# A two-block transformer on one core: the mixing input projection on split weights and rows, paired latent values, and a router in four column groups

## The reference, cut to what matters

```python
# first_block, layer 0: latent attention, 8 heads, values of 64 columns
kv = jnp.einsum('bsr,rhd->bshd', rms_norm(c_kv, kv_lat_norm), w_ukv)
k_nope, v_a = kv[..., :MLA_NOPE], kv[..., MLA_NOPE:]
o_a = dense_causal_attention(q, k, v_a)
...
# second_block, layer 0: the mixing layer; w_in is 1024 x 3072, ctx has 256 rows too
h = modulate_2(rmsnorm(x, g_mix), sh1, sc1)
z = h @ w_in[i]
q, k, v = jnp.split(z[..., 3 * C_HYENA:], 3, axis=-1)      # 3 * C_HYENA = 1536
hc = modulate_2(rmsnorm(xc, g_mix), csh1, csc1)
kvc = hc @ w_in[i][:, kv_off:]                             # kv_off = 2048
kc, vc = jnp.split(kvc, 2, axis=-1)
y_na = neighborhood_attention(..., kc, vc, na_rpb[i])
y_hy = hyena_mixer(z[..., :3 * C_HYENA], *hy)              # short filter of 3 taps, long convolutions
x = x + gt1 * (jnp.concatenate([y_hy, y_na], axis=-1) @ w_mix_out[i])
...
# second_block, layer 1: mixture of 8 experts, 2 for each row
logits = (h @ w_router).astype(jnp.float32) + b_router.astype(jnp.float32)
top_val, top_idx = lax.top_k(logits, TOP_K)
```

## Time and profile before

| what | us |
| --- | --- |
| median of 3 runs (lowest to highest) | 2389.74 (2387.16 to 2394.24) |
| the profiled execution | 2388.43 |
| span in its trace | 2387.1 |
| busy: PE | 2295.7 (96%) |
| busy: DVE | 1800.2 (75%) |
| busy: ACT | 1226.5 (51%) |
| busy: POOL | 411.0 (17%) |
| mean granted clock of PE | 0.99 |
| transferred | 630.36 MB, mean 264 GB/s |

### The profile page before, as it was taken

The page is one execution under the profiler, slowest core; times in us unless marked ns, Lnnn a source line. Parts: engine busy times, 40 slices in busy tenths (PEclk is TensorE's granted clock), DMA queues, the critical chain, the costliest instruction groups (busy, mean ns, idle before and its releaser), DMA issues.

```text
span 2387.1 us, 27392 instructions
## 1 busy us (share of the span) xinstructions
PE 2295.7 (96%) x10949; PEld 1734.8 (73%) x10949; DVE 1800.2 (75%) x2024; ACT 1226.5 (51%) x1436; POOL 411.0 (17%) x447
## 2 busy tenths in 40 slices
PE   6988999999999999899999899999999999999998
PEld 2455897545599877447996588788887888788886
DVE  4756787687698855675664388989888888889897
ACT  1243653223255321334433377777767676767775
POOL 1234570134165010452220000000000000000000
PEclk9999999999999999999999999999999999999999
DMA  8633568541647874134664379989998999899995
GB/s 328 251 156 106 229 256 314 221 192 72 220 177 282 322 304 185 53 142 176 247 247 172 115 290 361 353 333 358 355 361 327 361 356 355 328 369 352 366 352 216
DMA packets 49463, 630.36 MB, mean 264 GB/s; under 512 B 7456, under 2 KB 8049, under 8 KB 11633
## 3 DMA queue, kind: packets, MB, share of 16 engines
q1 hardware_dynamic: 44192, 618.81, 68.6%
q10 hardware_dynamic: 2752, 6.99, 0.8%
q0 software_dynamic: 2384, 2.73, 0.3%
...
## 4 chain that ended last, share of the span: by engine, by line
PE 82%; DVE 10%; ACT 3%; issue 2%; DMA 2%; POOL 1%; ACTq 0%; SPq 0%; DVEq 0%
PE psum L1198 19%; PE psum L1199 19%; PE psum L1200 19%; PE psum L1064 5%; PE psum L1093 4%; PE psum L2655 3%; DVE sbuf L727 2%; DVE ring_r L1193 2%; PE psum L2658 1%; PE psum L3276 1%; DVE sbuf L1340 1%; DMA ring<-in_t_ada 1%; PE psum L2316 1%; PE psum L3176 1%; DMA ring<-in_t_mlp 1%
## 5 line engine op out<-in xcount | busy, mean ns | idle before, releaser
L1199 PE MATMUL psum<-ring_r,sc_r 128*128 128x512 f32 x1688 | 665.1, 394 | 0.0
L1193 DVE TENSOR_TENSOR ring_r<-ring,sbuf_r 128x2048 fp32r<-128x2048 f32 (+1 forms) x287 | 536.7, 1876 | 141.2 <-ACT sbuf_r L1184 139.7
L1184 ACT CAST sbuf_r<-ring 128x2048 fp32r<-128x2048 f32 (+1 forms) x287 | 445.6, 1556 | 313.3 <-PE psum L1200 255.9
L1193 DVE TENSOR_TENSOR ring_r<-ring,sc_r 128x2048 fp32r<-128x2048 f32 (+1 forms) x243 | 476.2, 1969 | 107.3 <-ACT sc_r L1184 106.5
L1184 ACT CAST sc_r<-ring 128x2048 fp32r<-128x2048 f32 (+1 forms) x243 | 398.3, 1643 | 246.6 <-PE psum L1200 224.2
L1198 PE MATMUL psum<-sbuf_r,sc_r 128*128 128x512 f32 (+1 forms) x1148 | 425.6, 371 | 3.5 <-DVE ring_r L1193 3.1
L1199 PEld LDWEIGHTS psum<-ring_r,sc_r 128*128 128x128 f32 x1688 | 316.9, 188 | 72.0 <-issue 1.4
L727 DVE SCALAR_TENSOR_TENSOR sbuf<-ring,sbuf 128x512 f32<-128x512 f32 x405 | 332.7, 828 | 15.0 <-DMA ring<-in_t_ada 9.5
L1200 PE MATMUL psum<-sbuf_r,sc_r 128*128 128x512 f32 x860 | 339.6, 395 | 0.0
L1198 PE MATMUL psum<-sc_r 128*128 128x512 f32 x828 | 331.1, 400 | 0.0
L1200 PE MATMUL psum<-sc_r 128*128 128x512 f32 x828 | 324.3, 392 | 0.0
...
## 6 DMA issues: line engine op xcount, KB each, us to landing
...
```

The source lines that it names most:

```text
L1184: p.act.e.copy(p.r(hi), src).then_inc(*p.sig("high", st.tag, n))
L1193: p.dve.e.tensor_tensor(p.r(src), src, p.r(hi), ALU.subtract).then_inc(*p.sig("lowp", st.tag, n))
L1199: e.matmul(out, l[0], r[1], start=False, stop=False)
```

## The change

Three edits, in one diff.

**The input projection of the mixing layer.** The weight is cut into 24 pieces. Pieces 0 to 19 are 8 row blocks by 128 columns, four to a tile; pieces 20 to 23 are 2 row blocks by 512 columns. ACT casts each piece into one of three buffers (`HBI`, two of which are the normed rows' own buffer `XN`), GpSimd subtracts it in place (`pool_in2`), and PE does three products where there was one. The rows `n4` and the context rows are split as well (`HTLI`, `HTCL`, `FTI`). Pieces 16 to 19 serve two units each, and pieces 20 to 23 serve all four units 12 to 15, which therefore all finish with the last piece. Unit ends are now told by `in2_done`. ACT waits for the last piece of the MLP (`piece mlp1 63`) and casts piece 0 before the norm; each later cast stands three pieces ahead in ACT's list. ACT's context turn stands behind piece 7, and its 12 activations for the short filter are dealt out over tile 3's pieces. The load of the spectra `KH` goes behind all six rounds, and POOL's seeds of the tiles 41 to 43 stand between its subtractions.

**The values of the latent attention.** The heads are paired, with four `PT` buffers, and `pe_pair_values` skips the masked half of the second key block.

**The router.** Its weights are padded to 32 columns; the eight products go to four column groups of 32, two per group. The four parts are added by the matmul that used to transpose, with a matrix `SEL` of four stacked identities that DVE makes ahead. Constant matmuls fill PE's waits. The subtraction for the rows' low parts goes from DVE to GpSimd, at the end of its list.

```diff
...
         self.mla = mla = Heads("mla", [sc[:, 13824 + 256 * i:14080 + 256 * i] for i in range(4)],
-                               [xn[:, 512 * i:512 * i + 512] for i in range(2)], [(i,) for i in range(4)], [(4,), (5,)], 3,
-                               dil.DG)
+                               [xn[:, 512 * i:512 * i + 512] for i in range(4)], [(i,) for i in range(4)], [(4,), (5,)], 3,
+                               dil.DG, pair=True)
         for h in range(8):
-            mla.causal(self, h, h % 2, QT[0:96, h, :], KT[0:96, h, :])
-            mla.rows(h, 2, 64, [KV[:, k, 128 * h + 64:128 * h + 128] for k in range(2)], v3(mla.PT[h % 2], 2), [6, 7],
+            mla.causal(self, h, h % 4, QT[0:96, h, :], KT[0:96, h, :])
+            mla.rows(h, 2, 64, [KV[:, k, 128 * h + 64:128 * h + 128] for k in range(2)], v3(mla.PT[h % 4], 2), [6, 7],
                      HT[:, h // 2, :], False)
...
         self.HTC = v3(sc[:, 11288:13336], 8)
+        self.HTLI, self.HTCL = v3(sc[:, 15236:17284], 8), v3(sc[:, 17284:19332], 8)
+        self.FTI = [sc[:, 8216 + 256 * i:8472 + 256 * i] for i in range(4)]
+        self.HBI = [sc[:, 19332:20356], XN[:, 0, :], XN[:, 1, :]]
...
         self.HBE = [sc[:, 16112:18160], sc[:, 18160:20208], self.ht, self.acc]
-        self.RWL, self.RW = sc[:, 0:64], v3(sc[:, 0:64], 8)
-        self.BR = sc[:, 64:72]
+        self.RWL, self.RW = sc[:, 0:256], v3(sc[:, 0:256], 8)
+        self.BR = sc[:, 256:264]
+        self.SEL = sc[:, 15528:15536]
...
 def turn_at(p, tag, r):
-    return p.at("turnA" if r % 2 == 0 or tag in LOW else "turnD", tag, r)
-LOW = ("n1", "n3", "n5")
+    return p.at("turnA", tag, 2 * r + 1) if tag in LOW else p.at("turnD" if r % 2 else "turnA", tag, r)
+LOW = ("n1", "n3", "n4", "n5", "ctx")
...
-def act_turn_low(p, tag, tmp, mul, add):
+def act_turn_low(p, tag, tmp, mul, add, banks=TURNS):
     for c in range(8):
...
             p.act.wait_ge(*p.at("low", tag, c - len(tmp)))
-        p.act.e.activation(tmp[c % len(tmp)], p.bank[TURNS[c // 2]][:, 256 * (c % 2):256 * (c % 2) + 256], ACT.Identity,
+        bank = p.bank[banks[c // 2 % len(banks)]]
+        p.act.e.activation(tmp[c % len(tmp)], bank[:, 256 * (c % 2):256 * (c % 2) + 256], ACT.Identity,
                            bias=add[:, c:c + 1], scale=mul[:, c:c + 1]).then_inc(*p.sig("turnA", tag, c))
...
     if f"n{s}" in LOW:
-        act_turn_low(p, f"n{s}", p.FTF if s == 5 else p.FTM, mul, add)
+        act_turn_low(p, f"n{s}", {4: p.FTI, 5: p.FTF}.get(s, p.FTM), mul, add)
     else:
...
     if f"n{s}" in LOW:
-        dve_turn_low(p, f"n{s}", p.FTF if s == 5 else p.FTM, p.HT, p.HTLF if s == 5 else p.HTLM)
+        dve_turn_low(p, f"n{s}", {4: p.FTI, 5: p.FTF}.get(s, p.FTM), p.HT, {4: p.HTLI, 5: p.HTLF}.get(s, p.HTLM))
     else:
...
         for h in pair:
-            ins = p.pe.e.matmul(p.bank[h.bank][h.r0:h.r0 + h.v[kb].shape[1], 0:256], h.v[kb], h.pt[:, kb, :],
+            q0 = 0 if (h.both or kb % 2 == 0) else 128
+            ins = p.pe.e.matmul(p.bank[h.bank][h.r0:h.r0 + h.v[kb].shape[1], q0:256], h.v[kb], h.pt[:, kb, q0:256],
                                 start=(kb == 0), stop=(kb == n - 1))
...
     return p.at("in2A" if u % 2 and not 6 <= u < 12 else "in2D", u)
+def in2_done(p, u):
+    if u < 8:
+        return p.at("piece", "win2", 2 * u + 1)
+    return p.at("piece", "win2", {10: 17, 11: 19, 15: 23}[u]) if u in (10, 11, 15) else p.at("in2", u)
+def in2_stream(p):
+    return Stream("win2", pieces(range(5), False, lambda t: 8, 512, 1024) + pieces((5,), True, lambda t: 8, 512, 1024),
+                  p.HBI, lambda t: (8, 512))
 def pe_in2(p):
-    e, HT = p.pe.e, p.HT
+    HT, HTC = (p.HT, p.HTLI), (p.HTC, p.HTCL)
+    st = in2_stream(p)
     for j in range(6):
...
+        for q in range(4):
+            n = 4 * j + q
+            hi, lo = st.parts(p, n)
+            hi, lo = p.r(hi), p.r(lo)
+            p.pe.wait_ge(*p.at("scaled", "win2", n))
+            units = (2 * j + q // 2,) if j < 4 else (8 + q // 2, 10 + q // 2) if j == 4 else (12, 13, 14, 15)
+            for u in units:
+                ps = p.bank[2 + u % 5]
+                i = u - IN2_U[j]
+                tag, rows = ("n4", HT) if i < 2 else ("ctx", HTC)
+                if u >= 5 and (q == 0 if j == 5 else q % 2 == 0):
+                    p.pe.wait_ge(*in2_at(p, u - 5))
+                if j < 5:
+                    for k in range(8):
+                        p.pe.wait_ge(*p.at("low", tag, k))
+                        ins = three(p, ps[:, 256 * (q % 2):256 * (q % 2) + 256], (hi[:, k, :], lo[:, k, :]),
+                                    [p.r(r[:, k, :]) for r in rows], k == 0, k == 7)
+                    if j == 4 and q % 2 and i < 2:
+                        ins.then_inc(*p.sig("in2", u))
+                else:
+                    b = i % 2
+                    for k in range(2 * q, 2 * q + 2):
+                        ins = three(p, ps, [p.r(r[:, k, 128 * b:128 * b + 128]) for r in rows],
+                                    (hi[:, k - 2 * q, :], lo[:, k - 2 * q, :]), k == 0, k == 7)
+                    if q == 3 and u < 15:
+                        ins.then_inc(*p.sig("in2", u))
+            ins.then_inc(*p.sig("piece", "win2", n))
         if j:
             pe_sums(p, 36 + j)
         if j == 1:
...
-def put_in2(p, E, side, j):
+def put_in2(p, E, side, units):
     banks = in2_banks(p)
-    for u in range(IN2_U[j], IN2_U[j + 1]):
+    for u in units:
         if 6 <= u < 12:
...
             if side == "A":
-                E.wait_ge(*p.at("in2", u))
+                E.wait_ge(*in2_done(p, u))
                 E.e.activation(p.r(hi), ps, ACT.Copy, scale=scale).then_inc(*p.sig("in2A", u))
...
             ps = v3(p.bank[2 + u % 5], 2) if double else p.bank[2 + u % 5]
-            E.wait_ge(*p.at("in2", u))
+            E.wait_ge(*in2_done(p, u))
             ins = E.e.tensor_copy(dst, ps) if side == "D" else E.e.copy(dst, ps)
...
 def act_mix(p):
     a, e = p.a, p.act.e
+    st = in2_stream(p)
+    p.act.wait_ge(*p.at("piece", "mlp1", 63))
+    act_high(p, st, 0)
     act_norm(p, 4)
     e.dma_start(p.CX, a["ctx_2"][0].rearrange("(b p) d -> p b d", p=128)).then_inc(*p.land("ctx_in"))
     act_modulated(p, 4)
+    p.act.wait_ge(*p.at("tp", "n4", 3))
+    act_high(p, st, 1)
+    act_high(p, st, 2)
     act_context(p)
+    p.act.wait_ge(*p.at(*mod_at(p, 2, 0, 1)))
+    p.act.wait_ge(*p.at(*mod_at(p, 2, 1, 1)))
+    for n in range(24):
+        j, q = n // 4, n % 4
+        act_high(p, st, n + 3)
+        if q % 2:
+            put_in2(p, p.act, "A", (n // 2,) if j < 4 else (8 + q // 2, 10 + q // 2) if j == 4 else
+                    (12, 13, 14, 15) if q == 3 else ())
+        if q == 3 and j:
+            act_gates(p, 36 + j)
+        if n == 7:
+            p.act.wait_ge(*p.at("low", "n4", 7))
+            act_turn_low(p, "ctx", p.FTI, p.CTXC[1], p.CTXC[0], [0, 1])
+        if j == 3:
+            if q == 0:
+                p.act.wait_ge(*in2_at(p, 4))
+                p.act.wait_ge(*in2_at(p, 5))
+                p.act.wait_ge(*p.at("shorts"))
+                p.act.wait_ge(*p.at("low", "ctx", 7))
+            for c in range(3 * q, 3 * q + 3):
+                e.activation(p.ZC[:, c, :], p.ZT[:, c, 0:256], ACT.Identity, bias=p.SB[:, c:c + 1],
+                             scale=p.SW[0][:, c:c + 1]).then_inc(*p.sig("left", c))
     p.act.wait_ge(*p.total("kept0"))
     p.act.wait_ge(*p.total("kept1"))
     e.dma_start(p.KH, p.spectra.rearrange("p (m n) -> p m n", m=5)).then_inc(*p.land("kh_in"))
-    p.act.wait_ge(*p.at(*mod_at(p, 2, 0, 1)))
-    p.act.wait_ge(*p.at(*mod_at(p, 2, 1, 1)))
-    for j in range(6):
...
     act_gates(p, 42)
     put_hz(p, p.act, "A")
     act_exp(p, p.na, 0)
...
     for j in range(6):
-        put_in2(p, p.dve, "D", j)
+        put_in2(p, p.dve, "D", range(IN2_U[j], IN2_U[j + 1]))
         dve_products(p, 8, 37 + j)
...
         if j == 1:
-            dve_turn(p, "ctx", p.HTC, 8, [0, 1], p.CTXC[1], p.CTXC[0])
+            dve_turn_low(p, "ctx", p.FTI, p.HTC, p.HTCL)
         if j == 3:
...
+def pool_in2(p):
+    st = in2_stream(p)
+    pool_seed(p, 40)
+    for n in range(24):
+        hi, src = st.parts(p, n)
+        p.pool.wait_ge(*p.at("high", "win2", n))
+        p.pool.e.tensor_tensor(p.r(src), src, p.r(hi), ALU.subtract).then_inc(*p.sig("scaled", "win2", n))
+        pool_seed(p, {12: 41, 16: 42, 20: 43}.get(n, 0))
 def pool_mix(p):
-    pool_seed(p, 43)
+    pool_in2(p)
     for i, one, two, end in steps(p.na):
...
         p.pe.wait_ge(*ht_at(p, 7, k))
-        ins = e.matmul(p.bank[2][0:8, 0:256], p.RW[:, k, :], p.HT[:, k, :], start=(k == 0), stop=(k == 7))
+        g = 32 * (k % 4)
+        ins = e.matmul(p.bank[2][g:g + 32, 0:256], p.RW[:, k, :], p.HT[:, k, :], start=(k < 4), stop=(k >= 4))
     ins.then_inc(*p.sig("logits"))
+    pe_constants(p, 6, (256,))
+    p.pe.wait_ge(*p.at("select"))
     p.pe.wait_ge(*p.at("turnedlogits"))
     for b in range(2):
```

(22 more changed lines are left out.)

40 lines of the change are left out of this document (4 added, 36 removed).

## The result

The changed kernel takes 2416.85 us (median of 4 runs, 2412.96 to 2421.47) against 2388.99 for the kernel before: 1.0107 times, 95% interval 1.0088 to 1.0126. The direction was forecast, the size was not: +27.9 us where +8.2 was predicted, and 2416.85 lies above the range's end of 2410. The profiled execution has a span of 2417.2 us against 2387.1, so 30.1 us are to be found in its trace.

A forecast was written before the change was run, and what follows sets the result against it. PE was taken to bound the kernel. Terms from -20.1 to +10.6 gave +9.7 us for the mixing stage, -1.5 latent values, 0 router: +8.2 on 2389.7, 2398 us; range 2378 to 2410.

The forecast's parts named there:

- Columns: Mixing input projection: three split products take PE less time than one float32 product, 20.1 us less.
- The shared way as exclusive: Mixing stage, path into SBUF: a two-input DVE operation waits until GpSimd's ends, and the reverse; three places cost 19.7 us.
- costs little: Rival, mixing stage: GpSimd and DVE hardly hold each other up, the three places' 19.7 us fall away; 2374 us, chance 0.20.
- Piece 11: Mixing stage, round 2: its cast waits behind ACT's context turn and DVE's context splits, so the round ends 6.7 us late.
- The tail: Mixing stage, last product to attention scores: DVE's last adaLN products come late, 7.0 instead of 2.8 us, +4.2 us.
- Router: Router: column groups and fills gain, GpSimd's row subtraction blocks DVE's small steps; 0 taken, bounds -4.3 to +2 us.
- The norm ahead of it: +3.5 us: Norm before the mixing projection: ACT waits for the last MLP piece and casts piece 0 before squaring, +3.5 us.
- Split rows: Mixing stage's start: splitting the rows delays the first piece, +2.4 us; one split held by a subtraction, another +2.4.
- place 2: Mixing stage, context split: it stands behind DVE's products for tiles 36 and 37, round 2 ends near 906, +6.7 us.
- GpSimd as bound: Rival, mixing stage: subtractions of 2.94 us are slower than PE, whose clock falls after idling; 2410 us, chance 0.15.
- Latent values: -1.5 us: Latent attention: paired heads save PE time, 0 to 2.6 us, 1.5 taken, kept because its stage sets the end.
- Place 3: Mixing stage, round 5: banks are cleared only after DVE's products and short-filter steps, PE's second unit starts late, +10.6 us.

The follow-up runs named there:

- e8: Kernel before with the mixing edit alone, DVE subtracting, its work dealt out and products a round earlier, cast of piece 0 behind the norm: 2377.81 us (0.9942).
- e4: Changed kernel with the 24 subtractions on DVE instead of GpSimd, adaLN products and short filter dealt out over pieces: 2405.15 us (1.0052).
- e11: e7 with seven of eight adaLN products left out for tiles 37 to 42: 2392.31 us (1.0006).
- e5: Changed kernel with constant matmuls in four of PE's waits of the mixing stage: 2421.68 us (1.0121).
- e6: Changed kernel with the wait for the last MLP piece and the cast of piece 0 behind the norm in ACT's list: 2413.71 us (1.0095).
- e3: Kernel before with the mixing projection edit alone: 2415.87 us (1.0100).
- e2: Kernel before with the router edit alone (column groups, fills, row subtraction on GpSimd): 2391.51 us (1.0002).
- e9: Kernel before with the paired latent values and small constant matmuls in the same loop: 2392.75 us (1.0005).
- e12: e8 and e9 in one kernel, plus the router edit with its row subtraction on DVE behind the choice of experts: 2381.14 us (0.9948).
- e1: Kernel before with the paired latent values alone: 2394.54 us (1.0016).
- e7: Changed kernel, GpSimd still subtracting, with DVE's list dealt out evenly and adaLN products a round earlier: 2410.08 us (1.0077).

## Why the prediction was wrong in size

**What held.** *Columns:* in rounds without a wait the split form runs as reckoned (e8: rounds 4 and 5 in 45.4 us against 55.4), and e8 collects 13.7 us of the 20.1 at the scores. *The shared way as exclusive:* the case on which the sign was staked. e4, e8 and e11 show it from three sides, and the rival "costs little" is out. *One subtraction:* 2.35 us predicted; the 24 take 2.35 to 2.84, half of them at most 2.41. *Piece 11:* PE waited 5.2 us for it, part of the 6.7. *The tail:* 7.2 us from the last product to the scores, 7.0 predicted. *Router:* +0.5 for 0.

The Trainium skill, SBUF — State Buffer, SBUF: two separate sides, gives the rule: whoever starts first of a GpSimd operation and a DVE operation with two SBUF inputs or in a two-port mode gets the port pair for the whole instruction. This trace agrees, with 2.77 us for a product of 0.75. Its section Who interferes with whom also names copy, cast and tensor_scalar as operations that can be such and `tensor_reduce` as never one; here the rows agree too (1.97 for 0.49, 2.46 for 0.29, and 0.17 for the reduction L3109 inside a subtraction).

**Step that failed, in the stage: "The norm ahead of it: +3.5 us" and "Split rows" with one held split, +2.4.** I let GpSimd hold only operations with two inputs. Its first subtraction also held the scaling of the norm (L896, 1.97 us for 0.49). PE's fill matmuls before the second transposes ran at 1.2 GHz and took 3.6 us instead of 1.9, and the transposes came 6.4 us late instead of 3.5. Pieces 1 and 2 then held two steps of the splits, the cast and the subtraction, and PE stalled for 4.2 us where the sum had 2.4. At the end of round 1 the change is 9.4 us behind, where the prediction's times had 3.8. This is 5.6 of the 8.4 us by which the stage was undersized; 2.1 more are the gap between the prediction's times and its sum. Apart from that, the steps of place 2 (900.5, then 1.0, 1.05, 2.35 and 2.85) end at 907.8, not at 906.

**Step that failed, behind the waits: the clock.** I put the 1.2 GHz level only into the rival of GpSimd as bound. It came without that rival. PE's second unit of round 5 started at 110.3 us in the table's time, 3.6 later than forecast, and the rest of the round took 23.7 us instead of 21.1. Nothing for the part between scores and router was the other half: 4.8 us there, of which e5, with PE kept busy before the scores, gives back 3. The time of that part, from the scores to the last norm's reciprocal, goes with the time that its clock is low in all fourteen profiles: 386.8 us with 6.8 us at the 1.2 GHz level (the kernel before), 388.3 to 388.6 with 10.2 us (five), 388.7 to 389.5 with 13.7 (five), 391.6 with 19.2 (the changed kernel and e6) and 393.3 with 20.7 (e3). The four profiles without a mixing edit take 388.3 to 389.3, so 1.5 to 2.5 of the 4.8 us belong to the profile of the kernel before and not to the change.

The rival of GpSimd as bound was also added up wrongly: its terms, 16 x 0.65, 6 and twice 2, make 20.4 and not 12, which is 2418 and not 2410. The range's upper end rests on the 12. The measured 2416.85 lies near 2418 by luck: the rival's cause, a subtraction of 2.94 us, did not come.

**Step that failed, in sign: "Latent values: -1.5 us".** I kept the gain with the words "Its stage sets the end (same row)". The same row has DVE busy for 9.46 of 10 us and PE for 8.81: over the whole stage DVE is busy 26.1 of 29.8 us, with and without pairs, and PE had 6.4 us to spare. So the stage had nothing to give: it takes 29.8 us without pairs (before, e2, e8), 30.3 with filled pairs (e9, e12) and 30.6 to 30.7 with bare ones. Why filled pairs are still 0.5 longer no run isolates. The idle that the bare pairs open also lowers the clock over the projection behind, 15.5 us for 14.0. Together this is +2.5 in the trace and +3.1 by medians in e1 (0.04 to 0.29%).

**What is not the change's.** 1.7 us before the stage and 2.4 in the experts lie in code that no edit touches. The expert part takes 1010.8 to 1013.8 us in all profiles but e4's (1017.3). How much of that is chance in one profile stays open.

**Place 3, "+10.6".** It was right in sum only: a wait of 1.6 us at round 3's sum and one of 6.3 in round 5, and 2.6 of clock. The better sum would have been a single one. In the stage DVE and GpSimd need the shared way for 59.6 us (subtractions), 36.0 (products), 11.6 (short filter) and 11.4 (row and context splits): 118.6 us, where PE's pieces keep it busy for 94.4 in e8 and 94.8 in e11. With DVE subtracting in 1.22 us it is 88.3. With 13 products in place of 48 (e11) it is 92.4. That one comparison tells which of e7, e8 and e11 follow PE, without a model of the queues; only the stalls of e4 need the order.
